# Expert layers: each head's routing two head steps ahead of its dots, with the second and third head routed inside the first step

## The reference, cut to what matters

```
def chunk(xc):                                   # 128 tokens at a time
    q = (xc @ w_q).reshape(128, 8, 2, 128)
    s = einsum('thid,hikd->thik', q, sub_keys)
    s1, i1 = top_k(s[:, :, 0], 16); s2, i2 = top_k(s[:, :, 1], 16)
    cand = s1[..., :, None] + s2[..., None, :]   # 16 x 16 per token and head
    top_s, pos = top_k(cand, 16)
    eidx = take_along_axis(i1 * 128 + i2, pos)
    gate = softmax(top_s)
    hid = gelu(einsum('td,thkd->thk', xc, u_emb[eidx]))
    return einsum('thk,thkd->td', gate * hid, v_emb[eidx])
```

## Time and profile before

| what | value |
|---|---|
| median of the runs (3 runs, 3717.32 to 3719.09) | 3717.59 us |
| the profiled execution, its own time | 3710.72 us |
| span of the profile | 3709.4 us |
| mean granted TensorE clock | 0.921 |
| PE busy | 3054.5 us (82%) |
| DVE busy | 1963.8 us (53%) |
| POOL busy | 1535.5 us (41%) |
| ACT busy | 366.9 us (10%) |
| mean DMA rate | 305 GB/s |

### The profile page before, as it was taken

How to read it: one execution, slowest core, us unless ns; L and a number is a source line. 1 busy time by engine, 2 the same in 40 slices (tenths; PEclk the granted TensorE clock), 3 DMA queues, 4 the chain that set the end, 5 groups by cost and what they waited for, 6 DMA issues and landing times.

```text
span 3709.4 us, 31258 instructions
## 1 busy us (share of the span) xinstructions
PE 3054.5 (82%) x11602; PEld 1345.9 (36%) x11602; DVE 1963.8 (53%) x4441; ACT 366.9 (10%) x935; POOL 1535.5 (41%) x1587
## 2 busy tenths in 40 slices
PE   8999897879988878678878789887655656689999
PEld 4484546224533325323323223546111111135444
DVE  0051457777766644666666534456666666513223
ACT  1000321120000001000000001231000000002212
POOL 0010004656556554566666661003666666620000
PEclk9999998889999989888989999998888888899999
DMA  6274229999999997899999997527999999973242
GB/s 275 89 289 185 93 102 343 368 319 382 412 412 399 387 412 281 343 412 407 412 407 412 409 412 315 203 95 292 395 379 356 358 369 359 369 278 135 92 159 80
DMA packets 261505, 1130.78 MB, mean 305 GB/s; under 512 B 29796, under 2 KB 37188, under 8 KB 242280
## 3 DMA queue, kind: packets, MB, share of 16 engines
q0 software_dynamic: 221184, 805.40, 56.0%
q1 hardware_dynamic: 35496, 315.97, 21.8%
q10 hardware_dynamic: 4672, 7.41, 0.5%
HBM read 1120.20 MB, written 8.46 MB: 304 GB/s over the span
## 4 chain that ended last, share of the span: by engine, by line
PE 41%; DVE 22%; DMA 18%; issue 6%; POOL 6%; another core or an unknown queue 5%; ACT 2%; SPq 0%; DVEq 0%; ACTq 0%; POOLq 0%
DVE big L2572 10%; DMA big<-in_u,xT 10%; PE ps L1064 8%; PE ps L2379 7%; DMA big<-in_v,xT 7%; PE ps L242 6%; POOL big L2616 5%; PE ps L2294 3%; PE ps L1617 2%; PE ps L724 1%; PE ps L1172 1%; PE ps L1183 1%; PE ps L1760 1%; DVE smallu L2451 1%
## 5 line engine op out<-in xcount | busy, mean ns | idle before, releaser
L2379 PE MATMUL ps<-big,bc 128*32 128x512 f32 x3072 | 1046.8, 687 | 361.1 <-DMA big<-in_v,xT 258.8
L2572 DVE CUSTOM_DVE_ANT_0 big<-big,ps 128x1024 f32<-128x1024 f32 x768 | 920.1, 1214 | 277.9 <-DMA big<-in_u,xT 209.0
L2616 POOL DMA_INDIRECT big<-in_u,xT x768 | 730.6, 951 | 585.2 <-issue 197.2
L2616 POOL DMA_INDIRECT big<-in_v,xT x768 | 730.4, 951 | 404.9 <-issue 195.2
L2379 PEld LDWEIGHTS ps<-big,bc 128*32 128x32 f32 x3072 | 192.2, 118 | 1091.1 <-issue 540.6
L1064 PE MATMUL ps<-w,xT 128*128 128x512 f32 x768 | 340.4, 600 | 6.3 <-DMA w<-in_w_in 3.4
L242 PE MATMUL ps<-w,xT 128*128 128x512 f32 x512 | 223.8, 597 | 2.8 <-ACT xT L521 1.2
L1064 PEld LDWEIGHTS ps<-w,xT 128*128 128x128 f32 x768 | 145.8, 193 | 184.9 <-issue 176.0
L2294 PE MATMUL ps<-tmp,w 128*128 128x256 f32 (+1 forms) x832 | 183.6, 382 | 20.7 <-issue 18.1
L2294 PEld LDWEIGHTS ps<-tmp,w 128*128 128x128 f32 x832 | 155.8, 209 | 46.2 <-issue 24.6
L592 POOL TENSOR_TENSOR small<-small 128x32 f32<-128x32 f32 (+1 forms) x8 | 33.2, 4154 | 298.8 <-DVE small L563 238.5
(11 more groups left out here) (371 smaller groups left out, 3219.3 us busy)
## 6 DMA issues: line engine op xcount, KB each, us to landing
w<-in_w_in SPq DMA_DIRECT2D x58, 2048.0 KB
bc<-in_w_mod SPq DMA_DIRECT2D x20, 2048.0 KB, 10.5
w<-in_w_conv SPq DMA_DIRECT2D x24, 1536.0 KB
w<-in_peer_wq SPq DMA_DIRECT2D x12, 2048.0 KB
w<-in_w_out SPq DMA_DIRECT2D x10, 2048.0 KB
w<-in_conv_out_w SPq DMA_DIRECT2D x6, 2048.0 KB
big<-in_u,xT POOLq DMA_INDIRECT x768
big<-in_v,xT POOLq DMA_INDIRECT x768
```

The lines of the kernel that those rows point to most:

```text
L2379: ins = pe.e.matmul(self.ps[32 * g:32 * g + 32, 2 + half, :], p["diag"][part % 2][:, 256 * g + 32 * m:256 * g + 32 * m + 32], p["ring"][:, ...
L2572: dve.inc(dve.e.tensor_tensor_reduce(out=row, in0=row, in1=p["xc"], scale=1.0, scalar=0.0, op0=ALU.mult, op1=ALU.add, accum_out=p["hid"][t ...
L2616: ins = pool.e.indirect_dma_start(p["ring"][:, slot, :], None, table, bass.IndirectOffsetOnAxis(index, 0))
```

## The change

The routing of a head is moved one head step further ahead: step s routes the head of step s + 2. Head 1 is no longer routed before the first dot; in step 0 the routings of head 1 and head 2 are chained and run two pieces behind each dot, from the first dot on. On PE, the scores for step s + 2 are made at the third u place of step s, in step 0 at u place 8 (second call: 4). The indices of a part are turned in the part's even step at u place 8 and copied by DVE after dot 12, in step 0 at 14 and after dot 15, instead of at the first dot of the odd step. PE's turn now also waits for "ranked" of the head after the next. The four queries of tile 1 that use chunk 0 of the weights move behind queries 4 and 5, which head 2 needs. ACT's exponentials follow two ahead.

```
     def query_items(self, stream):
         if stream:
             return [(i, 0, 2) for i in range(16)]
-        return [(i, tile, tile + 1) for tile in range(2) for i in range(4)] + [(i, 0, 2) for i in range(4, 16)]
+        both = [(i, 0, 2) for i in range(4, 16)]
+        return [(i, 0, 1) for i in range(4)] + both[:2] + [(i, 1, 2) for i in range(4)] + both[2:]
+
+    def ahead_of(self, stream, step):
+        if step:
+            return 2, 8, 12
+        return 4 if stream else 8, 14, 15
...
     (scores, PE)
-            if step >= 2:
-                pe.wait_ge(self.dve, name, "diag" if step % 2 else "eidxT", step // 2 - 1)
+            if step >= 3 and step % 2:
+                pe.wait_ge(self.dve, name, "eidxT", step // 2 - 1)
+            elif step >= 4:
+                pe.wait_ge(self.dve, name, "diag", step // 2 - 2)
...
     (turn_experts, PE)
             pe.wait_ge(self.dve, name, "experts", 2 * part + 1)
+            if 2 * part + 2 < STEPS:
+                pe.wait_ge(self.dve, name, "ranked", 2 * part + 2)
...
     (peer_pe)
-                step = e // TOPK
-                if e % TOPK == 0 and step % 2:
+                step, k = e // TOPK, e % TOPK
+                at_scores, at_turn, _ = self.ahead_of(stream, step)
+                if k == at_scores and step + 2 < STEPS:
+                    scores(step + 2)
+                if k == at_turn and step % 2 == 0:
                     turn_experts(part)
-                if e % TOPK == 2 and 0 < step < STEPS - 1:
-                    scores(step + 1)
...
     (peer_act)
-                if e == 6 or e % TOPK == 11 and 1 < e // TOPK + 1 < STEPS:
-                    self.gate_exp_act(act, name, p, e // TOPK + 1)
+                if e == (5 if stream else 6):
+                    self.gate_exp_act(act, name, p, 1)
+                if e % TOPK == 11 and e // TOPK + 2 < STEPS:
+                    self.gate_exp_act(act, name, p, e // TOPK + 2)
...
     (peer_dve)
-        alone(self.route_dve(dve, l, name, p, 1))
...
             if k == 0:
-                if step % 2:
-                    dve.wait_ge(self.pe, name, "experts turned", part)
-                    if part >= 2:
-                        dve.wait_ge(self.pe, name, "sum", 16 * (part - 2) + 15)
-                    dve.inc(dve.x.tensor_copy(p["eidxT"][part % 2], p["turnedE"]), name, "eidxT", part)
                 alone(routing)
-                routing = self.route_dve(dve, l, name, p, step + 1) if 0 < step < STEPS - 1 else iter(())
+                routing = self.route_dve(dve, l, name, p, step + 2) if step + 2 < STEPS else iter(())
+                if not step:
+                    routing = itertools.chain(self.route_dve(dve, l, name, p, 1), routing)
...
-            if k >= LAG:
-                next(routing, None)
+            for _ in range(1 if step else 2):
+                if k >= LAG or not step:
+                    next(routing, None)
+            if step % 2 == 0 and k == self.ahead_of(stream, step)[2]:
+                dve.wait_ge(self.pe, name, "experts turned", part)
+                if part >= 2:
+                    dve.wait_ge(self.pe, name, "sum", 16 * (part - 2) + 15)
+                dve.inc(dve.x.tensor_copy(p["eidxT"][part % 2], p["turnedE"]), name, "eidxT", part)
```

More of the change, by code:

```diff
@@ L1 @@
+import itertools
 import math
```

## The result

| what | before | after |
|---|---|---|
| median of the runs side by side on one chip | 3718.34 us (4 runs) | 3688.44 us (4 runs, 3685.24 to 3691.49) |
| ratio, 95% interval | | 0.9914 (0.9898 to 0.9929) |
| span of the profile | 3709.4 us | 3684.1 us |
| DVE busy, POOL busy | 1963.8, 1535.5 us | 1970.8, 1536.9 us |
| mean granted TensorE clock | 0.921 | 0.924 |

The changed kernel is faster by 29.9 us in the medians, by 25.3 us in the profiled executions. Its lines lie further down: the gather is L2633 (before L2616), the dot L2583 (L2572), the sum of v rows L2392 (L2379), the copy to eidxT L2592 (L2564), the first line of a routing L2461 (L2446), the exponentials L2457 (L2442), the last two lines of a routing L2501 and L2502 (L2486 and L2487).

What follows compares the result with a forecast made beforehand. It took DMA idle time at the calls' starts, where POOL waits for routing, as the thing to gain. 10 + 8 + 0 + 5 - 1 = 22 us off the 3717.6 us median gave 3695 us, range 3670 to 3714.

Steps and rivals of the forecast that it cites:

- The likeliest case: Whole kernel: the summed forecast holds, 3695 us within its own range of 3675 to 3711; chance 0.55.
- signs of being wrong: Dot 31 moves over 5 us, third call's settled rate changes over 10 GB/s, or position 48 is issued as before.
- Third start: Start of third call: u 32 no longer waits for routing, closing a 12.0 us DMA gap; 10 us gained, 7.5 to 12.
- Second start: Start of second call: the same with less cover, DMA gap 10.9 us, backlog put at 5; 8 us gained.
- First call: Start of first call: the 10-slot ring still waits for the first sum; 0 gained, between -3 and +5.4 us.
- Settled third call: Settled stretch of third call: POOL's 14.6 us of routing waits vanish, partly replaced by slot waits; 5 us, 0 to 14.6.
- The moved eidxT copy: Head of odd steps: DVE's stall for PE moves by two dots to the wait for scores and stays; 0 gained.
- The weights' chunk: Chunk 2 of the weights, issued some 7 us later: PE waits 0 to 1 us, up to 3; -1 in sum.
- POOL beside DVE: POOL's gather issues: 0.94 us whether DVE does dots or routing pieces, so no stretching by these operations.
- A: Starts of calls: full slots and PE's sums give the gain back, leaving 7 us, 3711 us; chance 0.17.
- B: Settled third call: without routing waits 360 becomes 390 GB/s, total gain 42 us, 3676 us; chance 0.14.
- C: Late PE completions ahead of head 2's scores hold DVE at dot 4 for 13.7 us; 19 slower, 3736 us; chance 0.14.

Runs made afterwards that it cites:

- e1: Changed kernel's steps 0 and 1, but nothing routed in step 2 and one head ahead from step 3; 3687.96 us, 0.9943 to the kernel before.
- e2: Steps 0 and 1 as in the kernel before, new query order, heads 3 and 4 in step 2, then two ahead; 3712.83 us, 1.0009 to before.
- e4: Changed kernel with the old order of queries in the first and third call; 3691.20 us, 0.9946 to the kernel before.
- e6: Changed kernel with nothing routed in step 1, heads 3 and 4 both in step 2; 3688.51 us, 0.9939 to the kernel before.
- e12: Changed kernel, first call one ahead from step 3, second call's head 3 routed in step 2 with head 4; 3681.15 us, 0.9894 to before.
- e11: Changed kernel, but the third call routes one head ahead again from step 3; 3695.68 us, 0.9931 to the kernel before.
- e8: Changed kernel with indices again turned and copied at the first dot of the odd step; 3687.52 us, 0.9938 to the kernel before.
- e7: Changed kernel, routing pieces from behind the sixth dot, not third, from step 1; indices copied at the last dot; 3686.84 us, 0.9928 to before.

## Why the prediction was right

I forecast 3695 us and 22 us of gain; it was 3688.4, 29.9 in the medians and 25.3 in the profiled executions. The later sets gave 25.5 and 30.2, so the 8 us beyond the forecast are in part what sets differ by. The likeliest case came true, and e1 shows that its main ground, the start, carries most of it.

One of my own signs of being wrong stands all the same: the third call's rate in the window of the earlier trace rows went from 360 to 372 GB/s, by more than 10. It says little, as the window slides over the call when the call begins earlier: 183 us behind the first gather the rates are 360 before and 366, 361 and 367 in the three executions with the changed schedule.

- **Third start, 10 us (7.5 to 12).** 8.5 at position 48 and 11.9 at position 64. DVE's path came out almost line by line: dot 0 at +8.4 us (forecast 8.3), u 16 at +25.2 (25), dot 31 at +85.8 (87). Two details were off. The exponentials came 5 us sooner than worked out (a wait of 3.0 us, not 7.8). I had put a narrow query at half of a wide one and so the new order at 1.8 us later; it made them 3.6 us earlier (30.6 to 27.0), as ACT's second copy comes about 24 us behind the first gather with either order, and what counts is how much is still to be made then. The slack returned as waits for scores (3.0 and 3.7 us), so the error did no harm. I gave the reorder no gain of its own. By position 48 of single executions it is worth some 5 us alone (e2), the routing alone 7.9 (e4) and both 8.5: they take away much the same wait, and that my sum held was in this respect luck. The other detail: the DMA share did not stay at 0.9 up to dot 31. In step 1 POOL runs at the pace of DVE's dots with their pieces, which is slower than a gather, 0.77 for 16 us.
- **Second start, 8 us.** 8.0 at position 48, 12.1 by the last gather. The further 4.1 us are within what the settled part scatters by (688.9 to 694.9 us in the runs with that start, e6 and e12 aside). The value rested on an estimated backlog, and no run measured that by itself. I had not seen that there the price of head 3 lies open: e6 and e12 show 10 us at position 48. Dot 16 came 3.9 us later there (forecast 2 to 4), and dot 31 all the same 1.9 us earlier.
- **First call, 0 (-3 to +5.4).** 0.5: 3.1 us at position 48 and 2.7 back behind it, within scatter.
- **Settled third call, 5 us (0 to 14.6).** 6.3 behind position 48, but 3.6 of that lie ahead of position 64 and belong to the start, as e1 and e11 have them too. The 2.7 from there on are within scatter, so that this match is luck as far as one pair of traces goes; the averages of all executions say 8. The waits for the routing's last line are gone from it (14.6 to 0.3 us). e2's median seemed to say 0, but it holds a loss in the first call of its own.
- **The moved eidxT copy, 0.** Its waits fell from 171 us over the span to 11.8, and those before the first line of a routing went from 184 to 166; I had expected these to grow. e8 shows that it is worth a few us at most.
- **The weights' chunk, -1 us.** The wait was 1.6 us in the first call and 5.0 in the third, over the 3 that I had as its end, but dot 31 of e4 shows that it is covered: the price is 0 there.
- **POOL beside DVE.** I had read that DVE's pieces never stretch a gather's issue. The rows that I went by show 0.94 us, but the whole traces do not bear it out. In the changed kernel 52 of the 1536 gathers took more than 1.05 us on POOL, up to 2.01, and beside each of them DVE ran a TENSOR_TENSOR or SCALAR_TENSOR_TENSOR, operations with two tensor inputs; of the 1245 gathers with none of these beside them the longest took 1.02. In 21 of the 52 it was one of the two 128x512 multiplications of a routing:

```profile
939.00 0.69 DVE L2492 TENSOR_TENSOR xT<-xT,small 128x512 f32<-128x512 f32 x1
939.06 1.45 POOL L2633 DMA_INDIRECT big<-in_u,xT  x1 [1.46 <-PE ps L2392]
939.72 0.69 DVE L2493 TENSOR_TENSOR xT<-xT 128x512 f32<-128x512 f32 x1
```

  Beside those multiplications the excess over 0.94 us is 7.2 us over the span, and in the kernel before 8.7 (23 gathers), so the change neither pays nor gains by it, and the price of 0 was right. But the box on DVE blocking DMA in the Trainium skill, "SBUF — State Buffer", was set aside too soon: it speaks of fast modes of DVE, and whether these operations run in one no run here shows; but gathers that DVE holds up are what it tells of, and they are here.
- **The rates.** The settled second call moves 412 GB/s, the third 366 to 372. Both are over the 358 that the Trainium skill, "DMA: Bandwidth & Descriptors", gives as the limit from HBM in its section on where 436 GB/s comes from. That figure is a stack's rate divided by two cores, and this kernel runs on one, so the measurement rules it out as the ceiling here and says nothing against it for two cores at work.
- **The rivals.** A (the ring gives it back) shows in the second call, as the 4.5 us of idle DMA behind 1516, where POOL waits for PE's first sum; it took none of the gain that I had counted. B (360 becomes 390 GB/s) did not come: 366 in the like stretch, and e7 took most of the waits for scores away without it. C (late completions hold the scores of head 2) did not occur in the three executions of the changed kernel: dot 31 of the third call was at 84.4 to 85.9 us in each.

## What to carry over

Routing further ahead helps where a stream starts, for there the engine that makes the indices has nothing to hide behind; in the settled stream the same edit is worth a few us or none, and single traces scatter by as much. Each call has its own second in line (here PE's queries in the third, DVE's extra head in the second), so a schedule that is the same for all calls leaves time in some of them: with one per call (e12) the gain over the changed kernel was 9.2 us more. Half of a change is rarely clean: e2's settled half carried a catching up of its own and the new order of the queries besides, one hiding a gain and the other adding one. And a change that reorders work has two parts: here the order of six queries, thought of as a cost, moved ACT's exponentials 3.6 us forward.

## What the runs showed of the chip

PE made no steady progress in places where the DMA engines moved 410 GB/s or more. In e6, from 2572 to 2589 us, only 8 matmuls are recorded, 1.4 to 2.8 us apart with nothing that they wait for, and ACT got two queries in 18.3 us that else come 3.46 us apart; the pace was back at 2589, within 5 us of POOL's last gather before its stop. The kernel before has such a stretch in its third call, with matmuls 2.1 to 2.8 us apart. A third place is likely the start of the third call, where ACT's second query copy comes 23.7 to 23.9 us behind the first gather in all fourteen executions. Records can be missing from a trace, but the queries are late by ACT's clock too. The granted clock is not the cause: in e6 it was 0.98 from 2572 to 2577 us, with three matmuls of 0.38 us in that time, and fell to 0.50 only after it. I had read this as completions that reach the other engines late; e6 speaks rather for a PE that issues slowly. What slows it was not tried and stays open.

POOL's cadence of gathers without a wait was 1.24 us. By the rate of the second call the DMA engines need 1.28 us for one, so by this estimate a queue once empty fills up again by only 0.04 us for each gather.
